# Splitting the first weight units of the second out projection in eight pieces inside the attention steps

## What is computed

```python
# second layer
p_lat = h_lat @ odd_w_in[i]                  # 1024 -> 2560
p_ctx = h_ctx @ odd_w_in[i]
a_lat, _ = na_mixer(p_lat[..., :1536], p_ctx[..., :1536], na_rpb[i], False)
b_lat, _ = gqa_mixer(p_lat[..., 1536:], p_ctx[..., 1536:], gqa_q_g[i], gqa_k_g[i], False)
y_lat = jnp.concatenate([a_lat, b_lat], axis=-1) @ odd_w_out[i]    # 1024 -> 1024
# inside na_mixer, for each grid row r of 64 queries
s_loc = einsum('bhqd,bhkd->bhqk', qi, kr) * scale + bias           # 512 local keys
s_loc = where(mask, s_loc, NEG_INF)
s_ctx = einsum('bhqd,bhkd->bhqk', qi, kc) * scale                  # 256 context keys
p = softmax(concatenate([s_ctx, s_loc], axis=-1))
o = p[..., :n_ctx] @ vc + p[..., n_ctx:] @ vr
```

## Time and profile before

| | |
|---|---|
| median of 3 runs | 1773.92 us (1773.48, 1773.92, 1778.62) |
| the profiled execution | 1778.1 us, of which the span 1776.4 |
| TensorE busy | 1690.2 us, 95% of the span |
| VectorE busy | 1026.4 us, 58% |
| ScalarE busy | 643.3 us, 36% |
| GpSimd busy | 278.0 us, 16% |
| chain that ended last | TensorE 84%, VectorE 5%, ScalarE 3%, DMA 3% |
| busy from 1188.0 to 1208.6 | TensorE 13.53 of 20.60 us, mean granted clock 0.67 |
| busy from 1208.6 to 1252.0 | TensorE 41.42 of 43.40 us, clock 1.00; VectorE 31.96 |

### The profile page before, as it was taken

One profiled execution on the slowest core, in us unless ns is written; L12 is line 12 of the kernel. 1 busy time (PEld: TensorE's weight loads), 2 busy tenths in 40 slices (PEclk: granted clock), 3 DMA queues, 4 the chain that ended last, 5 costly groups with the idle time before them and its releaser, 6 DMA issues.

```text
span 1776.4 us, 26976 instructions
## 1 busy us (share of the span) xinstructions
PE 1690.2 (95%) x10042; PEld 1354.4 (76%) x10042; DVE 1026.4 (58%) x1938; ACT 643.3 (36%) x1090; POOL 278.0 (16%) x394
## 2 busy tenths in 40 slices
PE   5899899999999999999999999999999999999996
PEld 1777566668898888888878778876678888888885
DVE  2666565763747777777775681257653644444453
ACT  2413555663421212212234342245543433233351
POOL 0423332330300000000000031145420300000000
PEclk9999999999999999999999999999999999999998
DMA  8579532275623343443342443362403443331233
GB/s 302 180 240 306 139 85 49 46 94 171 199 57 96 98 139 108 129 120 117 100 153 93 177 166 136 118 179 60 129 10 114 136 117 97 94 94 60 94 131 118
DMA packets 265528, 224.27 MB, mean 126 GB/s; under 512 B 75224, under 2 KB 226136, under 8 KB 265432
## 3 DMA queue, kind: packets, MB, share of 16 engines
q1 hardware_dynamic: 257370, 206.42, 39.3%
q0 software_dynamic: 6048, 14.87, 2.2%
q10 hardware_dynamic: 2016, 1.71, 0.3%
HBM read 193.71 MB, written 29.25 MB: 126 GB/s over the span
## 4 chain that ended last, share of the span: by engine, by line
PE 84%; DVE 5%; ACT 3%; DMA 3%; issue 2%; SPq 1%; POOL 1%; ACTq 0%; DVEq 0%
PE ps L1252 30%; PE ps L852 11%; PE ps L854 10%; PE ps L853 10%; PE ps L1047 5%; PE ps L1129 5%; PE ps L1092 4%; PE ps L1262 2%; PE ps L1084 1%; PE ps L909 1%; ACT arena L1552 1%; PE ps L1236 1%; PE ps L1237 1%; PE ps L1238 1%; DMA wide_raw<-in_ada_w 1%
## 5 line engine op out<-in xcount | busy, mean ns | idle before, releaser
L852 PE MATMUL ps<-w_hi,act_hi 128*128 128x512 f32 (+2 forms) x952 | 368.6, 387 | 2.4 <-DVE act_lo L1750 1.3
L854 PE MATMUL ps<-w_hi,act_lo 128*128 128x512 f32 (+2 forms) x952 | 364.1, 382 | 0.0
L853 PE MATMUL ps<-w_lo,act_hi 128*128 128x512 f32 (+2 forms) x952 | 364.0, 382 | 0.0
L1750 DVE TENSOR_TENSOR w_lo<-w_raw,w_hi 128x2048 fp32r<-128x2048 f32 (+4 forms) x114 | 206.8, 1815 | 248.1 <-ACT w_hi L1401 247.4
L1252 PE MATMUL ps<-act_lo,w_hi 128*128 128x512 f32 (+1 forms) x912 | 277.9, 359 | 0.0
L1252 PE MATMUL ps<-act_hi,w_hi 128*128 128x512 f32 (+1 forms) x912 | 276.2, 357 | 0.0
L1252 PE MATMUL ps<-act_hi,w_lo 128*128 128x512 f32 (+1 forms) x912 | 274.4, 355 | 0.0
L1401 ACT ACTIVATE w_hi<-w_raw 128x2048 fp32r<-128x2048 f32 (+3 forms) x108 | 168.5, 1561 | 269.5 <-PE ps L854 234.5
L852 PEld LDWEIGHTS ps<-w_hi,act_hi 128*128 128x128 f32 x952 | 179.1, 188 | 42.2 <-issue 8.8
L854 PEld LDWEIGHTS ps<-w_hi,act_lo 128*128 128x128 f32 x952 | 179.0, 188 | 33.9
L853 PEld LDWEIGHTS ps<-w_lo,act_hi 128*128 128x128 f32 x952 | 179.2, 188 | 32.5
(11 more groups left out here) (129 smaller groups left out, 2019.3 us busy)
## 6 DMA issues: line engine op xcount, KB each, us to landing
arena<-in_ada_w SPq DMA_DIRECT2D x44, 1024.0 KB, 9.0
w_raw<-in_ffn_up SPq DMA_DIRECT2D x88, 512.0 KB, 5.3
w_raw<-in_ffn_down SPq DMA_DIRECT2D x88, 256.0 KB, 3.0
w_raw<-in_odd_w_in SPq DMA_DIRECT2D x20, 512.0 KB, 4.5
arena<-mods SPq DMA_DIRECT2D x16, 512.0 KB, 6.4
proj_odd<-arena POOLq DMA_DIRECT2D x26, 256.0 KB, 2.5
x_after_mix<-arena SPq DMA_DIRECT2D x10, 512.0 KB, 2.9
arena<-x_after_mix SPq DMA_DIRECT2D x10, 512.0 KB, 5.2
```

Source lines behind the costliest of these rows:

```text
L852: mm(out_, s_hi, m_hi, start=start, stop=False)
L853: mm(out_, s_hi, m_lo, start=False, stop=False)
L854: return mm(out_, s_lo, m_hi, start=False, stop=stop)
L1750: V.tensor_sub(out_, full, hi.bitcast(fp32)).then_inc(sem_, 1)
```

## The change

The splits of units 10 and 11 leave `in_projection` (for chunk 4 neither split(8) nor split(9) is issued), and `out_piece` gets the layer as an argument, so that NA's steps 1 to 8 split them in quarters as MLA's do in the first layer. `piece_hi` counts on from 6. TensorE, SyncE and GpSimd have the same instructions in the same order.

```diff
@@ ScalarE, in_projection
-                    split(2 * c)
+                    if c < 4:
+                        split(2 * c)
                     if layer and c == 0:
                         for s in range(2):
                             act.wait_ge(x_st[s], 16 * base("in1", "xs") // 2)
                     evict(c)
-                    split(2 * c + 1)
+                    if c < 4:
+                        split(2 * c + 1)
...
-            def out_piece(n, piece):
-                u, cols = base("out0", "w") + n, slice(512 * piece, 512 * piece + 512)
+            def out_piece(layer, n, piece):
+                u, cols = base(f"out{layer}", "w") + n, slice(512 * piece, 512 * piece + 512)
                 if piece == 0:
-                    act.wait_ge(mm_done, in_done(0, 6, NT - 1))
+                    act.wait_ge(mm_done, in_done(layer, 4 if layer else 6, NT - 1))
                     w_loaded(u)
                 A(w_hi[:, u % 2, cols], w_raw[:, u % 2, cols], ACT.Copy)                    .then_inc(w_hi_done if piece == 3 else piece_hi, 1)
@@ ScalarE, attention_stages
-                    if st.a.first and k in range(1, 9):
-                        out_piece((k - 1) // 4, (k - 1) % 4)
+                    if st.a.name in ("mla", "na") and k in range(1, 9):
+                        out_piece(int(st.a.name == "na"), (k - 1) // 4, (k - 1) % 4)
@@ VectorE, in_projection
-                    split(2 * c)
+                    if c < 4:
+                        split(2 * c)
                     chunk(c, 2 * c + 1)
-                    split(2 * c + 1)
+                    if c < 4:
+                        split(2 * c + 1)
...
-            def out_piece(n, piece):
-                u, cols = base("out0", "w") + n, slice(512 * piece, 512 * piece + 512)
+            def out_piece(layer, n, piece):
+                u, cols = base(f"out{layer}", "w") + n, slice(512 * piece, 512 * piece + 512)
                 if piece < 3:
-                    dve.wait_ge(piece_hi, 3 * n + piece + 1)
+                    dve.wait_ge(piece_hi, 6 * layer + 3 * n + piece + 1)
...
```

## The result

| | before | after |
|---|---|---|
| median, timed side by side (7 runs each) | 1778.62 us | 1782.01 us (1780.89 to 1785.31) |
| ratio | | 1.0029, 95% interval 1.0015 to 1.0042 |
| profiled execution, of which the span | 1778.1, 1776.4 | 1785.31, 1783.6 |

The changed kernel is 0.29% slower. The ratio is the one computed from all runs of both; it isn't the quotient of the two medians, which are 3.4 us apart (1.0019), while the means are 5.4 us apart. 1782.0 lies 1.5 us above the range. The direction was right (slower by less than 0.3%), the time was not.

A forecast was written before the change was run, and what follows sets the result against it. TensorE, busy 95% of the span, was taken as the bound, so only its standstills count. A passage gain of 2.25 us against 4.4 us for the pieces gave +2.1, from 1773.92 to 1776.0 us; 8-in-10 range 1771.5 to 1780.5.

The forecast's parts named there:

- The base: Whole kernel: +2.1 us put on the median of the runs shown, 1773.92 us, giving 1776.0 us.
- the +2.1 us: Whole kernel: net slowdown forecast, 4.4 us of cost for the pieces less 2.25 us gained at the passage.
- Split of unit 10 for nothing: Last chunk of the input projection: removing this split gains nothing, since TensorE runs through there.
- The gain at the passage, 2.25: Between second input projection and NA: without unit 11's split, masks finish sooner and scores(1) start 2.25 us earlier.
- The clock at the passage: Ahead of NA's scores(1): TensorE's clock was taken to fall as before, the new wait being 4.2 us; nothing counted.
- the 1.9 us of the rival: Passage: clock stays full through scores(1) and its transposes, up to 1.9 us more gain; total +0.2, 1774.1 us; chance 0.12.
- The eight pieces, 5.4 us before what is given back: NA turns 1 to 8: 0.45 + 2.0 + 0.3 + 0.3 + 2.0 + 0.35 us of cost.
- Given back at pair 3's tables, 1.0: NA turns 6 and 7: 1.0 us of their cost hidden in TensorE's waits for pair 3's bias tables.
- Cheap pieces: NA steps: 0.17 us a piece as in MLA, 1.4 us for eight; total −0.9, 1773.0 us; chance 0.25.
- GpSimd keeps the port: NA turns 4 and 8: VectorE's piece waits for scaling and mask, 2.08 us more each; +6.3, 1780.2 us; chance 0.13.
- No room at the front: Passage: masks stay at 5.80 us, gain only 0.6; total +3.8, 1777.7 us; inside the forecast's range, no separate chance.
- The chances: Whole kernel: faster by over 0.3% 0.03, slower by over 0.3% (over 1779.2 us) 0.11, within 0.86.

The follow-up runs named there:

- x4_tiny: Against the kernel before: unit 10 stays split whole, of unit 11 only 8 columns are split, in NA step 1 (for timing alone); ratio 0.9991 (0.9979 to 1.0003).
- x14_before: The kernel before, unchanged, profiled again; single execution 1778.21 us, from NA's first transposes to GQA's first scores 94.19 us.
- x5_extra_pieces: Against the kernel before: both whole splits stay and the eight pieces are made a second time in NA steps 1 to 8; ratio 1.0037 (1.0023 to 1.0050).
- x6_before_recip: Against the changed kernel: VectorE's pieces ahead of the step's second reciprocal, ScalarE's one turn earlier; ratio to the kernel before 1.0008 (0.9998 to 1.0018).

## Why the prediction was wrong, point by point

- **The base (the step that failed most).** I moved the +2.1 us from the profiled execution to the median of the three runs shown, 4.2 us lower, and so to 1776.0. Of those three runs two were 1773.48 and 1773.92, the third 1778.62. In five larger sets of runs the median of the kernel before was 1776.7 to 1778.6. Of the miss of 6.0 us, 4.7 are the base (1778.62 in the seven runs timed beside the change, not 1773.92) and 1.3 the distance of the medians (3.4 us, not 2.1). The profiled execution, 1778.1, would have been the better base: 1778.1 + 2.1 = 1780.2 is 1.8 us under the measured median instead of 6.0. That is luck, though: single executions of the kernel before ran from 1773.5 to 1785.2. With spells that come and go (3.84 or 6.12 us at 172, 1.5 us at 1404), three runs didn't fix the median to 4 us.
- **The size of the change (the second step that failed).** In the mean of 26 runs it is +4.9 us and not +2.1. The terms of the sum came out well one by one, as told below; what failed is that the sum had no term outside them. The spell inside NA, in two of six profiles, is 0.6 us; against the mean of five profiles of before NA costs 0.5 more than against the one that I read; and 2.1 us lie outside NA, of which 0.7 may be the spell near 1404 and the rest stays open.
- **Split of unit 10 for nothing.** Right: in x4_tiny it stays, and T to s1 is 9.14 us as with it gone.
- **The gain at the passage, 2.25.** Right by mechanism and size: 11.35 to 9.15 is 2.20, the masks take 4.12 us (4.16 foreseen), and they bound it. T to s1 isn't quite fixed in before, though: 10.82 to 11.39 us in the five profiles, 11.15 in the mean, so that the gain against the mean is 2.0.
- **The clock at the passage.** Half wrong. I let it fall as before and only then counted the longer wait. It stayed at 2.4 GHz through scores(0) and fell after the second wait; scores(1) still took 2.49 us, so that just 0.45 of the 1.9 us of the rival came (s1–s2 6.71 instead of 7.16).
- **The eight pieces, 5.4 us before what is given back.** In the table piece k shows in the spacing from s(k+2) to s(k+3): 0.49, 1.12, 0.96, 0, 0.47, 1.13, 0.96, and for the eighth −0.80 with the give-back. Foreseen were 0.45, 1.0, 1.0, 0.3, 0.3, 1.0, 1.0, and 0.35 − 1.0. The sum is 4.33 against 4.4. The place was told one turn too early: scores stand 5.69 us apart once in each group, not 5.5 in two turns running, and 5.05 and 7.04 around it.
- **Given back at pair 3's tables, 1.0.** Nothing beyond the ordinary step is left in any of the six profiles (s10–s11 5.83, as in x14_before). But what it was worth was read from one profile: s10–s11 of before is 6.63 there and 6.38 in the mean of five, so 0.55 us and not 0.8. With T to G of before also lower elsewhere, the net of NA is 2.2 us in the ordinary case and was 1.7 against the first profile.
- **What was left out, the spell in NA:** that a step stretched by pieces leaves TensorE waits after which its clock can fall inside NA, +1.65 us in two of six, 0.6 in the mean. It was in the earlier trace rows for the passage; I didn't ask it of the turns that I lengthened.
- **Rivals.** Cheap pieces: out, x5_extra_pieces has +3.8, and +4.3 from s2 on. GpSimd keeps the port: out, by the timeline of after in turn 8:

```profile
1257.80 1.85 POOL L2415 TENSOR_SCALAR arena<-arena,rinv 128x768 f32<-128x768 f32 x2
...
1259.00 1.18 DVE L1752 TENSOR_TENSOR w_lo<-w_raw,w_hi 128x512 fp32r<-128x512 f32 x1 [0.36 <-ACT w_hi L1546]
...
1259.61 2.52 POOL L2404 TENSOR_TENSOR arena<-arena,colmask 128x896 f32<-128x896 f32 x1
```

The piece takes 1.18 us, no more than elsewhere, though a mask is queued behind the scaling: the mask takes 2.52 us instead of 2.08. That fits VectorE having gone in between, though the mask's record starts before the piece ends. In eleven of the twelve such places of the six profiles (turns 4 and 8) piece and mask take these times. The Trainium skill (GPSIMD Engine Reference, section 8, Key points) has the contention and not this order. No room at the front: out, 4.12 us for the masks.
- **The chances.** Slower by over 0.3% got 0.11; the ratio is 1.0029 with 0.3% in the middle of its interval, so the 0.86 for "within" looks too sure; one case can't prove that.

## What to carry to other kernels

Before a change is timed against a median, look how far several profiles of the unchanged kernel differ and where; a few waits in untouched code can move it by more than the change. In these steps the pieces went best where their engine already waits for the same step's data (ahead of the reciprocal, with their input made a turn earlier: 4.57 us a step) and not behind it (5.69); which of the two moves did it wasn't parted. When a step of a loop gets longer on the feeding engine, price TensorE's clock too: behind the new waits it fell in 2 of 16 places here, for 1.65 us each.

## Not expected of the hardware

- The clock's fall is not decided by one wait of the kernel alone: the same 1.00 and 0.31 us waits ahead of s6 left it at 1.00 in four profiles and were followed by 1.2 GHz in two; at the second out projection it fell in 14 of 20 profiles.
- A VectorE subtraction of 512 columns with both inputs in SBUF took 0.67 us alone, 0.83 in x6_before_recip where GpSimd's scaling had begun 0.6 us earlier, 1.18 with the scaling 0.26 us old, and 1.69 under a mask of 2.09 us. In the last three it ended 0.54 to 0.55 us after the GpSimd instruction did. With a second GpSimd instruction queued, its 1.18 us didn't grow and the later one took 2.52 us instead of 2.08.
